# Expert products of a two-layer trunk on TensorE: three float32r products of high and low halves, or one float32 product on four 32-column tiles

## The reference, cut to what matters

```python
N_EXPERTS = 8
TOP_K = 2
def swiglu(x, w_gate, w_up, w_down):
    return (jax.nn.silu(x @ w_gate) * (x @ w_up)) @ w_down
def moe_swiglu(xn, w_router, w_gate, w_up, w_down):
    logits = (xn @ w_router).astype(jnp.float32)
    top_vals, top_idx = lax.top_k(logits, TOP_K)
    top_w = jax.nn.softmax(top_vals, axis=-1)
    combine = jnp.sum(jax.nn.one_hot(top_idx, N_EXPERTS, dtype=jnp.float32) * top_w[..., None], axis=-2)
    out = jnp.zeros_like(xn)
    for e in range(N_EXPERTS):
        out = out + combine[..., e:e + 1].astype(xn.dtype) * swiglu(xn, w_gate[e], w_up[e], w_down[e])
    return out
```

## Time and profile before

| what | us |
|---|---|
| median of 3 runs | 1786.49 |
| lowest, highest | 1781.48, 1786.92 |
| span of the profiled execution | 1782.2 |
| PE busy (share of the span) | 1720.8 (97%) |
| PE weight loads | 1373.5 (77%) |
| DVE, ACT, POOL busy | 1303.3, 1030.5, 253.4 |
| experts, from 754.0 to 1772.6 | 1018.6 |
| moved by DMA | 466 MB, mean 262 GB/s |

### The profile page before, as it was taken

How to read it: one execution, slowest core, us unless ns; L and a number is a source line. 1 busy time by engine, 2 the same in 40 slices (tenths; PEclk the granted TensorE clock), 3 DMA queues, 4 the chain that set the end, 5 groups by cost and what they waited for, 6 DMA issues and landing times.

```text
span 1782.2 us, 25682 instructions
## 1 busy us (share of the span) xinstructions
PE 1720.8 (97%) x9866; PEld 1373.5 (77%) x9866; DVE 1303.3 (73%) x1126; ACT 1030.5 (58%) x847; POOL 253.4 (14%) x338
## 2 busy tenths in 40 slices
PE   7889989999989999899999999999999999999997
PEld 7768989999989789867667667667677677676675
DVE  6557467445455765688788788788788888888887
ACT  5442344434454424377677677677676676676775
POOL 3877186000001650000000000000000000000000
PEclk9999989999999999899999999999999999999999
DMA  9602655555544027289899899899899899999993
GB/s 282 228 24 72 201 166 190 188 177 180 189 166 166 25 72 263 103 327 378 315 355 382 302 362 370 313 358 368 308 376 367 295 367 348 325 370 338 328 380 140
DMA packets 242786, 466.06 MB, mean 262 GB/s; under 512 B 9633, under 2 KB 91553, under 8 KB 242721
## 3 DMA queue, kind: packets, MB, share of 16 engines
q1 hardware_dynamic: 239808, 463.50, 72.7%
q0 software_dynamic: 416, 1.05, 0.3%
q10 hardware_dynamic: 2496, 0.61, 0.2%
HBM read 464.08 MB, written 1.05 MB: 261 GB/s over the span
## 4 chain that ended last, share of the span: by engine, by line
PE 90%; POOL 4%; DVE 2%; ACT 2%; issue 1%; ACTq 0%; DVEq 0%; POOLq 0%
PE work L582 62%; PE acc L582 22%; PE work L882 2%; PE work L845 1%; PE ssm_y L692 1%; PE work L683 1%; POOL arena L1573 1%; DVE arena L1179 0%; PE acc L653 0%; DVE parts L1161 0%; DVE xs L1168 0%; POOL arena L1572 0%; POOL arena L1568 0%; POOL arena L1569 0%; POOL arena L1571 0%
## 5 line engine op out<-in xcount | busy, mean ns | idle before, releaser
L1356 DVE TENSOR_TENSOR parts<-ring,parts 128x2048 fp32r<-128x2048 f32 x338 | 768.7, 2289 | 139.4 <-ACT parts L1096 138.8
L1096 ACT ACTIVATE parts<-ring 128x2048 fp32r<-128x2048 f32 x336 | 644.2, 1918 | 216.3 <-PE work L582 134.3
L582 PE MATMUL work<-parts,xs 128*96 128x512 f32 (+1 forms) x2880 | 669.9, 389 | 1.4 <-DVE xs L1423 1.4
L582 PEld LDWEIGHTS work<-parts,xs 128*96 128x96 f32 (+1 forms) x2880 | 452.1, 163 | 187.3 <-issue 5.0
L582 PE MATMUL work<-xs,parts 128*128 128x256 f32 x3648 | 463.8, 288 | 16.1 <-DVE xs L1168 13.9
L582 PEld LDWEIGHTS work<-xs,parts 128*128 128x128 f32 x3648 | 450.6, 194 | 27.3 <-issue 25.0
L1161 DVE TENSOR_TENSOR parts<-ring,parts 128x2048 fp32r<-128x2048 f32 x94 | 223.2, 2378 | 175.6 <-ACT parts L920 175.6
L582 PE MATMUL acc<-parts,hs 128*96 128x512 f32 x1344 | 319.9, 393 | 0.0
L582 PEld LDWEIGHTS acc<-parts,hs 128*96 128x96 f32 x1344 | 216.2, 161 | 92.6
L920 ACT ACTIVATE parts<-ring 128x2048 fp32r<-128x2048 f32 x94 | 179.1, 1910 | 121.2 <-PE work L582 68.8
L1012 ACT ACTIVATE sig<-work 128x256 f32<-128x256 f32 x48 | 18.4, 384 | 138.2 <-PE work L582 138.2
(11 more groups left out here) (230 smaller groups left out, 995.7 us busy)
## 6 DMA issues: line engine op xcount, KB each, us to landing
ring<-in_moe_w_gate SPq DMA_DIRECT2D x114, 1024.0 KB, 6.5
ring<-in_moe_w_up SPq DMA_DIRECT2D x112, 1024.0 KB, 6.8
ring<-in_moe_w_down SPq DMA_DIRECT2D x112, 1024.0 KB, 6.1
ring<-in_w_in SPq DMA_DIRECT2D x44, 1024.0 KB, 6.5
ring<-in_dense_w_gate SPq DMA_DIRECT2D x14, 1024.0 KB, 4.9
ring<-in_dense_w_up SPq DMA_DIRECT2D x14, 1024.0 KB, 4.9
ring<-in_dense_w_down SPq DMA_DIRECT2D x14, 1024.0 KB, 4.9
ring<-in_w_out SPq DMA_DIRECT2D x8, 1024.0 KB, 12.1
```

The lines of the kernel that those rows point to most:

```text
L582: last = nc.tensor.matmul(out_ap, a, b, start=start and n == 0, stop=stop and n == len(pairs) - 1, skip_group_check=shared)
L1096: nc.scalar.activation(parts[:, (S0 + j) % PARTS, 0, :], ring[:, n % RING, :], ACT.Copy)\
L1356: tt(parts[:, (S0 + j) % PARTS, 1, :], raw_unit(j), parts[:, (S0 + j) % PARTS, 0, :].bitcast(F32), ALU.subtract).then_inc(lo_ready, 1)
```

## The change

The expert part is rewritten; the stages before it keep their program.

- **No halves.** `xe` and `eh` are single float32 tensors. PE multiplies with the units as they arrive (`moe_view`, `moe_full`). ACT and DVE split no unit of an expert.
- **Four column tiles.** The 96 slots are three groups of 32. A matmul has 32 stationary columns and writes one 32-partition quarter of a bank. For gate and up there are 12 accumulators, 2 (gate, up) x 2 (column halves) x 3 (groups), in the quarters of three banks, `acc` 2 and 3 and `ssm_y`; for each k-tile 12 matmuls go through them in turn, x mod 4 being the tile. `down` has four column quarters x three groups, 12 matmuls of 256 columns for each k-tile, in three rounds of four (`OUT_ROUNDS`), into `acc` 0 and 1.
- **Sets.** The hidden columns are taken in sets of 1024 (three) and 512 (one), in the order gu0, gu1, d0, gu2, d1, gu3, d2, d3. A gate or up unit is 256 rows x 1024 columns, rows of 4 KB (of 2 KB in the last set).
- **14 slots.** `ring2` adds seven slots in the place of `br_slot` and `parts`. SP waits once for each pair of units, on `pair_used`, which PE raises.
- **Hidden rows.** They lie in quarters and halves of partitions. ACT takes silu in three pieces, DVE multiplies in two; `turn` transposes, for each 128 hidden columns, a full 128 x 128 block and a block of rows 64 to 127. The evacuation of `turn` is shared: ACT one half, DVE the other.
- **Combine.** `combine_rows(i)` runs inside item i after its first gate and up set and handles the result of item i - 1; for item 0 it adds zeros (`combine` and `y_tok` are zeroed first). After the loop `combine_rows(n_items)` handles the last. `y_tok` is filled by three copies of ACT and four of DVE.
- **SP's loops.** The first 14 units of item 0 are loaded ahead of the loop, those of item i + 1 at the end of item i's.

```diff
-    EXPERT = []
-    for c in range(NCH):
-        EXPERT += [f"G{2 * c}", f"G{2 * c + 1}", f"U{2 * c}", f"U{2 * c + 1}"]
-        EXPERT += [f"D{2 * c - 2}", f"D{2 * c - 1}"] if c else []
-    EXPERT += [f"D{NHC - 2}", f"D{NHC - 1}"]
...
+    SETS = [(0, 512), (1024, 512), (2048, 512), (3072, 256)]
+    NSET = len(SETS)
+    assert sum(2 * ns for base, ns in SETS) == FF
+    GU_PAIRS = [4 if ns == 512 else 2 for base, ns in SETS]
+    D_UNITS = [2 * ns // UC for base, ns in SETS]
+    ORDER = ["gu0", "gu1", "d0", "gu2", "d1", "gu3", "d2", "d3"]
+    EXPERT, PAIRS_AT = [], {}
+    for step in ORDER:
+        which = int(step[-1])
+        if step[0] == "g":
+            for n in range(GU_PAIRS[which]):
+                EXPERT += [("G", which, n), ("U", which, n)]
+        else:
+            EXPERT += [("D", which, n ^ 1) for n in range(D_UNITS[which])]
+        PAIRS_AT[step] = len(EXPERT) // 2
     IU = len(EXPERT)
+    PAIRS = IU // 2
+    MR = 14
+    OUT_COLS = D // 4
+    OUT_QUAD = [(0, 1, 2), (0, 1, 3), (2, 3, 0), (2, 3, 1)]
+    OUT_ROUNDS = [[(0, 0), (0, 1), (0, 2), (1, 2)], [(1, 0), (1, 1), (2, 0), (2, 1)],
+                  [(2, 2), (3, 2), (3, 0), (3, 1)]]
```

SP, `load_unit` and the loops:

```diff
+            def load_unit(j, e):
+                kind, which, n = EXPERT[j]
+                base, ns = SETS[which]
+                src = {"G": moe_gate, "U": moe_up, "D": moe_down}[kind]
+                w = (src[0, e:e + 1, :, :] if isinstance(e, int) else src[0, bass.ds(e, 1), :, :])
+                w = w.rearrange("a k n -> (a k) n")
+                if kind == "D":
+                    w = w[base + UC * n:base + UC * n + UC, :]
+                else:
+                    per = D // GU_PAIRS[which]
+                    w = w[per * n:per * n + per, base:base + 2 * ns]
+                sp.dma_start(moe_view(j), rows(w)).then_inc(moe_full[j % MR], 16)
+            def later_units(i, e):
+                for j in range(MR, IU):
+                    if j % 2 == 0:
+                        sp.wait_ge(pair_used, i * PAIRS + ((j - MR) // 2 + 1))
+                    load_unit(j, e)
+            def first_units(i, e):
+                for j in range(MR):
+                    if j % 2 == 0:
+                        sp.wait_ge(pair_used, i * PAIRS + ((j + IU - MR) // 2 + 1))
+                    load_unit(j, e)
+            for j in range(MR):
+                if j < RING:
+                    sp.wait_ge(lo_ready, S0 + j - RING + 1)
+                elif j == RING:
+                    sp.wait_ge(work_done, Group((DEPTH - 1, "gB", KT - 1)).done)
+                else:
+                    sp.wait_ge(work_done, Group((DEPTH - 1, "wo", KT - 1)).done)
+                load_unit(j, 0)
+            with sp.Fori(0, NE - 1) as i:
+                later_units(i, i)
+                first_units(i, i + 1)
```

PE:

```diff
+            def unit(j, i):
+                pe.wait_ge(moe_full[j % MR], i * (16 * PER_SLOT) + 16 * (j // MR + 1))
+                return moe_view(j)
+            def region(x, ns):
+                return gu_banks[x // 4][GRP * (x % 4):GRP * (x % 4) + GRP, 0:ns]
+            def gate_up(which, i):
+                ns, pairs = SETS[which][1], GU_PAIRS[which]
+                first = EXPERT.index(("G", which, 0))
+                per = KT // pairs
+                for n in range(pairs):
+                    gate, up = unit(first + 2 * n, i), unit(first + 2 * n + 1, i)
+                    for kk in range(per):
+                        k = n * per + kk
+                        for x in range(4 * NG):
+                            half, g = x % (2 * NG) // NG, x % NG
+                            w = gate if x < 2 * NG else up
+                            last = nc.tensor.matmul(region(x, ns), xe[:, k, g * GRP:g * GRP + GRP],
+                                                    w[:, kk, half * ns:half * ns + ns], start=k == 0,
+                                                    stop=k == KT - 1)
+                    last.then_inc(pair_used, 1)
+            def turn(which, i):
+                ns = SETS[which][1]
+                pe.wait_ge(erow_ready, i * 2 * NSET + (2 * which + 2))
+                per = ns // P // 2
+                for half in range(2):
+                    bank = begin(Group(("t", which, half), i), i)
+                    for q in range(per):
+                        f = half * per + q
+                        at = q * 2 * SLOTS
+                        nc.tensor.transpose(bank[:, at + P // 2:at + 2 * SLOTS],
+                                            erow[:, 1, f * P:f * P + P], ident[:, :])
+                        last = nc.tensor.transpose(bank[:, at:at + P // 2], erow[P // 2:P, 0, f * P:f * P + P],
+                                                   ident[P // 2:P, P // 2:P])
                     last.then_inc(work_done, 1)
+            def down(which, i):
+                first = EXPERT.index(("D", which, 1))
+                pe.wait_ge(eh_act, i * NSET + (which + 1))
+                pe.wait_ge(eh_dve, i * NSET + (which + 1))
+                for n in range(D_UNITS[which]):
+                    w = unit(first + n, i)
+                    for kk in range(UC // P):
+                        kt = (n ^ 1) * (UC // P) + kk
+                        begins = which == 0 and n == 0 and kk == 0
+                        ends = which == NSET - 1 and n == D_UNITS[which] - 1 and kk == UC // P - 1
+                        for quads in OUT_ROUNDS:
+                            for h, g in quads:
+                                q = OUT_QUAD[h][g]
+                                leads = h % 2 == 0 or (h, g) in ((1, 2), (3, 2))
+                                last = nc.tensor.matmul(
+                                    acc[GRP * q:GRP * q + GRP, h // 2,
+                                        (h % 2) * OUT_COLS:(h % 2) * OUT_COLS + OUT_COLS],
+                                    eh[:, kt, g * GRP:g * GRP + GRP],
+                                    w[:, kk, h * OUT_COLS:h * OUT_COLS + OUT_COLS],
+                                    start=begins and leads, stop=ends, skip_group_check=True)
+                    if n % 2:
+                        last.then_inc(pair_used, 1)
+            with pe.Fori(0, n_items) as i:
+                pe.wait_ge(xe_act, i + 1)
+                pe.wait_ge(xe_dve, i + 1)
+                gate_up(0, i)
+                combine_rows(i)
+                turn(0, i)
+                bank = begin(Group(("tw", 0), i), i)
+                pe.wait_ge(wpick_ready, i + 1)
+                for t in range(TT):
+                    last = nc.tensor.transpose(bank[0:SLOTS, t * P:t * P + P], wpick[:, t, :], ident[:, :])
+                last.then_inc(work_done, 1)
+                gate_up(1, i)
+                for which in range(1, NSET):
+                    down(which - 1, i)
+                    turn(which, i)
+                    if which < NSET - 1:
+                        gate_up(which + 1, i)
+                pe.wait_ge(pick_ready, i + 2)
+                gather("gather", i, 0)
+                gather("gather", i, 1)
+                down(NSET - 1, i)
+            combine_rows(n_items)
```

ACT and DVE in the loop (their splits are taken out):

```diff
+            def silu_gates(which, i):
+                ns = SETS[which][1]
+                act.wait_ge(pair_used, i * PAIRS + PAIRS_AT[f"gu{which}"])
+                low, high = slice(0, P // 2), slice(P // 2, P)
+                for dst, src in ((esilu[high, 0, 0:ns], gu_banks[0][low, 0:ns]),
+                                 (esilu[low, 1, 0:ns], gu_banks[0][high, 0:ns]),
+                                 (esilu[high, 1, 0:ns], gu_banks[1][low, 0:ns])):
+                    nc.scalar.activation(dst, src, ACT.Silu).then_inc(silu_set, 1)
+            def hidden_act(which, i):
+                half = SETS[which][1] // P
+                bank = arrived(Group(("t", which, 0), i))
+                turned = bank[:, 0:half * SLOTS].rearrange("p (f h n) -> p f h n", h=2, n=SLOTS)
+                dst = eh[:, 0:2 * half, :].rearrange("p (h f) n -> p f h n", h=2)[:, 0:half // 2]
+                nc.scalar.activation(dst, turned, ACT.Copy).then_inc(eh_act, 1)
...
-                def split_item(j):
-                    n = len(STREAM) + j
-                    act.wait_ge(slot_full[n % RING], i * (16 * IU // RING) + 16 * (n // RING + 1))
-                    if j >= PARTS:
-                        act.wait_ge(*item_used_up(EXPERT[j - PARTS], i))
-                    else:
-                        act.wait_ge(down_done, i * NHC + (NHC - PARTS + j + 1))
-                    nc.scalar.activation(parts[:, (S0 + j) % PARTS, 0, :], ring[:, n % RING, :], ACT.Copy)\
-                        .then_inc(hi_ready, 1)
...
+                for which in range(NSET):
+                    silu_gates(which, i)
+                    hidden_act(which, i)
...
             with dve.Fori(0, n_items) as i:
+                for which in range(NSET):
+                    hidden_product(which, i, 0)
+                    if which == 0:
+                        add_rows(0, i)
```

(12 more changed lines are left out.)

321 lines of the change are left out of this document (104 added, 217 removed).

## The result

The changed kernel takes **1802.1 us** (median of 4 runs, 1797.54 to 1804.69) where the kernel before took 1785.5 beside it: a ratio of 1.009, 95% interval 1.0076 to 1.0103. It is slower, by about 17 us, well clear of the 0.3% that can be told. The prediction had 1774 us, 12 less than before; its main case ended at 1792 us and its range at 1841. The profiled execution of after took 1804.69 us with a span of 1802.9, 20.7 longer than the span before.

The account below looks back on a forecast made before the run. The prediction took PE to bound the kernel, with DMA next. Its terms, -31 us in the experts, +19 at the loop's returns and +0.3 at the ends, gave -12 us: 1774 us, range 1715 to 1841.

Parts of the forecast that it names:

- main case: Whole kernel: four tiles overlap fully and returns to the loop top cost fetches; 1755 to 1792 us, chance 0.45.
- rival B: PE's feed in 256-column products slower than 54 ns per record; near end 1841 us, chance 0.20.
- What bounds the kernel: Expert part: PE, busy in 97% of the span, is the bound; DMA is second and the next limit.
- The products and the rest of PE's expert: Each expert on PE: products 108.6 us, in all 123.5 instead of 127.35, so 31 us less over eight.
- C: Column-tiled products: only two of four tiles run at once, 869 us more, about 2640; chance 0.06.
- The turns: Transposes of hidden rows: each change of tile shape drains PE, 0.15 us; 6.5 us per expert, 1.8 per eight.
- The wait at the combine: Combine after the next expert's first gate and up set: its 0.7 us wait goes, 0.3 us of PE wait put.
- The loop's back edge: PE's return to the loop top: waits for an instruction fetch, 2.7 us seven times, 19 us.
- Ends: Before the first and after the last expert: small effects of opposite sign, +0.3 us.
- The sum: Whole kernel: -31 + 19 + 0.3 = -12 us, put on the 1786.5 us median, giving 1774 us.
- The step on DMA: Expert weight loads: 357 GB/s asked, 366 to 392 available, so no wait of PE is exposed.
- The Trainium skill's rule: PE's loop body: instruction memory holds 2048 instructions, a taken branch to a missing page stalls, so the cost is not zero.

Follow-up runs that it names:

- experiment 7: Six weight slots instead of 14, on the changed kernel with PE's expert loop written out eight times: 1761.35 us, ratio 0.9866 to the kernel before.
- Experiment 6: Combine moved back to the end of its own expert, on the changed kernel with PE's loop written out: 1808.81 us, ratio 1.0127 to the kernel before.
- (2): Changed kernel with PE's expert loop body written out eight times, so no jump: 1759.56 us, ratio 0.9851 to the kernel before.
- (5): Kernel before, always-fulfilled waits added to PE's loop body: about 1,430 instructions 1787.76 us; 1,620 1785.07; 1,820 1826.48; 2,310 2154.05.
- experiment 1: Changed kernel with a hint on PE's expert loop that its closing branch will be taken: 1777.29 us, ratio 0.9946 to the kernel before.
- experiment 4: Changed kernel with the 12 matmuls of a gate and up k-tile issued tile by tile, not in rotation: 2058.56 us, one run.

## Why the prediction failed

- **The range.** 1802.1 us lies inside the stated range of 1715 to 1841, but by luck: the high end was set by rival B, which did not happen, and the main case, whose mechanism did, ended at 1792. The direction was wrong.
- **What bounds the kernel: right.** PE did before and does after; no run of the changed kernel shows it waiting for weights in the experts for longer than 1.0 us in all (experiment 7).
- **The products and the rest of PE's expert (123.5 us): right.** 123.01 measured without the jump. A k-tile takes 2.58 us (6 x 0.43), the down records of a whole set 10.36 / 192 = 0.054 us each, and four tiles overlap fully. The main gain was 8 x (127.35 - 123.0) = 35 us, 31 predicted. Rival B, a feed of PE slower than 54 ns per record, did not show, nor did C. By the rule that rival B names from the Trainium skill (TensorE: Matmul & The Clock Gate, Part 1) the down records would follow every 62 ns or so; the trace has 54. Either its condition, decoding that is not done in hardware, is not met here, or its figure is too high; in both cases it does not bound this kernel.
- **The turns: right.** 1.84 us for eight, 1.8 predicted; grouping them gave back 0.57 us each.
- **The wait at the combine: right, for more than it was priced at.** No wait of the combine or the first turn is left in an expert; the 0.3 us set for it are nothing. That the combine also covers the hidden product, and so keeps the clock up, the prediction had not seen: it listed the product only as a thing that might be late. Experiment 6 puts this placement at 49 us on the new code, the ninth combine counted against it: without it the change would have lost more.
- **The loop's back edge: the step that failed.** The mechanism was named, with its place and its packets, and its price was wrong: 2.7 us, "a single packet being nearer to that", seven times, 19 us. Measured are 3.8 us of standing still, with two packets of the program around the jump and not one, and on top some 2.5 us at half clock, which had no term at all. The experts' own lengths say 6.5 us a time (129.5 against 123.0), 45 us, 26 more than predicted. The slip behind it: the clock was read as 1.00 in every expert and taken as a constant, though there PE never stood still for more than 0.7 us at a time. Just ahead of the experts the trace of before has a stop of 1.93 us and, a little behind it, half clock (columns as in rows 2):

```profile
745.31:747.24 1.93, 0.00 (x0) 0.03 (x1) 1.74 (x10) 0.21 (x1) 0.00 (x0) 1.00 0.18 38
748.50:751.80 3.30, 3.30 (x18) 3.30 (x17) 1.92 (x7) 0.49 (x1) 0.00 (x0) 0.50 0.44 179
```

A step that brings a first long stop of PE has to be priced with the clock that it may lose. The prediction also counted the old body as 1150 instructions, where it has about 1,230; nothing hangs on that.
- **Ends: failed, in small.** +0.3 us predicted, about 7 measured: the ninth combine (5.4 us, in part at half clock) and the copies ahead of it (1.9), 7.3 us behind the last down product, where the 4.4 us of before were part of the eighth expert. A step moved into the next turn of a loop runs once more after it; if the first turn executes it as well, that is one execution more.
- **The sum.** Predicted -31 + 19 + 0.3 = -12; measured -35 + 45 + 7 = +17 to +18, the 18.3 us of the account above. The step on DMA was right in its outcome: 340 to 364 GB/s, nothing waits.
- **The Trainium skill's rule** on instruction memory (Runtime: NRT & Kernel Launch, Instruction fetch mechanics) gave the right sign for a body of 3,060. Its 2048 instructions are more than this kernel could use: a body of some 1,820 already stalled at six of its seven returns, one of 1,620 at none.

Shown by experiments: the gap and its clock are the loss (2), the gap needs only a long loop body (5), and the half clock comes with long stops of PE, without the jump it is gone (2) and stops of 2.7 us that have another cause bring it too (6). Not settled: which stops bring it, since some of 2.4 us (1) and of 3.2 to 3.4 us (4) did not; why the half-clock stretch is 3.4 us behind some and 6.8 behind others; why one of seven returns of the 1,820 body was free; and what exactly the jump waits for in its 3.8 us. Not tried: a loop body of two experts or one kept under 1,620 instructions, and a first expert without its combine.

## What to carry to other kernels

Count the instructions of the busiest engine's loop body before and after a change; when it passes the length that the kernel is known to keep, write the loop out or keep the body short, and price each return to the top at several microseconds of stop plus what the clock takes to come back. Where TensorE is the bound, most of its stops of 2.4 us and more cost more than their own length here, so work that can be placed into such a hole is worth more than its own length. Where tiles of TensorE work side by side, issue their records in rotation, and group instructions of one tile shape.

## What was not expected of the hardware

- Code that was fetched in 139 packets cost PE nothing when it ran straight on; 152 packets with seven jumps cost 45 us.
- A loop body of PE of 1,620 instructions came free, one of 1,820 cost 41 us over seven returns, of which one was free; the hint on the jump cut a gap from 3.8 to 2.2 us.
- TensorE's granted clock fell to 0.50 behind stops of 2.05, 2.37 and 2.86 us and stayed at 1.00 behind 1.74, 1.95, 2.35 and another 2.37 (experiment 1); with the tiles out of rotation it stayed at 1.00 behind four stops of 3.2 to 3.4 us (experiment 4).
- Four float32 streams on 32-column tiles cost no more than one: 0.43 us for four records of 512 columns, 0.054 us per record of 256 columns sustained over 192 records. Issued tile by tile, the same records made an expert 30 us longer.
- DMA engines that showed a busy share of 0.95 and of 1.02 moved the same 364 GB/s; the share did not tell how near the limit the transfers were.
